# An encoder kernel: the up-projection's weight blocks, with one block staged in PSUM and eight plain slots at the head

## The reference, cut to what matters

```
def conv_gated_mlp(h, w_up, conv_w, conv_b, w_down):
    up = h @ w_up                                   # (512, 1024) @ (1024, 5632)
    conv = sum(pad(up)[:, j:j + s] * conv_w[j] for j in range(3)) + conv_b
    a, b = jnp.split(conv, 2, axis=-1)
    return (jax.nn.gelu(a) * b) @ w_down

x = x + conv_gated_mlp(rmsnorm(x, g_ffn[l]), w_up[l], conv_w[l], conv_b[l], w_down[l])
```

## Time and profile before

| what | us |
|---|---|
| median of 3 runs (lowest to highest) | 1777.44 (1775.38 to 1779.08) |
| the profiled execution's own time | 1771.03 |
| its span | 1769.2 |
| TensorE busy | 1690.7 (96%) |
| VectorE busy | 1157.3 (65%) |
| ScalarE busy | 853.9 (48%) |
| GpSimd busy | 892.2 (50%) |

### The profile page before, as it was taken

The page is one execution under the profiler, slowest core; times in us unless marked ns, Lnnn a source line. Parts: engine busy times, 40 slices in busy tenths (PEclk is TensorE's granted clock), DMA queues, the critical chain, the costliest instruction groups (busy, mean ns, idle before and its releaser), DMA issues. The chain is left out here.

```text
span 1769.2 us, 24563 instructions
## 1 busy us (share of the span) xinstructions
PE 1690.7 (96%) x9161; PEld 1467.7 (83%) x9161; DVE 1157.3 (65%) x1644; ACT 853.9 (48%) x1535; POOL 892.2 (50%) x784
## 2 busy tenths in 40 slices
PE   9999999999995999999999999999999859999998
PEld 7888888888875999988888888888888759999886
DVE  5778875433368899972146887745333788999822
ACT  5766743223353566652256756432224636666423
POOL 3433433333476788853343433334335668888522
PEclk9999999999997999999999999999999979999999
DMA  8322232223231222243252222222332412333332
GB/s 262 108 78 90 72 119 73 95 95 142 96 119 48 96 96 96 96 145 100 92 187 96 72 78 90 96 96 92 97 143 76 139 48 80 101 100 103 132 113 77
DMA packets 147319, 182.78 MB, mean 103 GB/s; under 512 B 3040, under 2 KB 130706, under 8 KB 146194
## 3 DMA queue, kind: packets, MB, share of 16 engines
q1 hardware_dynamic: 147090, 181.35, 30.7%
q10 hardware_dynamic: 128, 0.09, 0.0%
HBM read 170.92 MB, written 10.50 MB: 103 GB/s over the span
## 5 line engine op out<-in xcount | busy, mean ns | idle before, releaser
L616 POOL TENSOR_TENSOR w_lo<-raw,w_hi 128x256 fp32r<-128x256 f32 x596 | 472.9, 828 | 740.6 <-ACT w_hi L718 740.6
L1814 PE MATMUL banks<-xg_hi,w_hi 128*128 128x512 f32 x768 | 302.3, 394 | 9.4 <-DVE w_lo L1259 9.4
L1815 PE MATMUL banks<-xg_lo,w_hi 128*128 128x512 f32 x768 | 300.5, 391 | 0.0
L1816 PE MATMUL banks<-xg_hi,w_lo 128*128 128x512 f32 x768 | 300.2, 391 | 0.0
L1259 DVE TENSOR_TENSOR w_lo<-raw,w_hi 128x768 fp32r<-128x768 f32 (+2 forms) x110 | 97.3, 885 | 167.8 <-ACT w_hi L717 167.6
L666 POOL TENSOR_TENSOR s_lo<-s,s_hi 128x1024 fp32r<-128x1024 f32 x72 | 194.7, 2725 | 13.5 <-ACT s_hi L1024 13.5
L1814 PEld LDWEIGHTS banks<-xg_hi,w_hi 128*128 128x128 f32 x768 | 145.1, 189 | 40.2 <-DVE w_lo L1259 11.0
L2049 PE MATMUL banks<-h_set,s_hi 128*128 128x256 f32 x576 | 148.3, 289 | 28.3 <-ACT banks L1034 15.1
L1816 PEld LDWEIGHTS banks<-xg_hi,w_lo 128*128 128x128 f32 x768 | 144.9, 189 | 30.5
L1815 PEld LDWEIGHTS banks<-xg_lo,w_hi 128*128 128x128 f32 x768 | 145.2, 189 | 28.8 <-issue 0.2
L717 ACT ACTIVATE w_hi<-raw 128x768 fp32r<-128x768 f32 (+2 forms) x111 | 80.6, 726 | 174.8 <-PE banks L1816 86.0
(11 more groups left out here) (247 smaller groups left out, 4250.2 us busy)
## 6 DMA issues: line engine op xcount, KB each, us to landing
raw<-in_w_in SPq DMA_DIRECT2D x55, 1024.0 KB, 5.1
raw<-in_w_up SPq DMA_DIRECT2D x44, 1024.0 KB, 5.1
raw<-in_w_br SPq DMA_DIRECT2D x16, 1024.0 KB, 4.9
raw<-in_w_down SPq DMA_DIRECT2D x12, 1024.0 KB, 5.0
x_spill<-x_res SPq DMA_DIRECT2D x4, 2048.0 KB, 7.6
x_res<-x_spill SPq DMA_DIRECT2D x4, 2048.0 KB, 9.2
raw<-in_w_out SPq DMA_DIRECT2D x8, 1024.0 KB, 4.9
raw<-in_w_down SPq DMA_DIRECT2D x8, 896.0 KB, 4.6
```

What stands on the lines that cost most here:

```text
L616: last = nc.gpsimd.tensor_tensor(w_lo[p_][:, k, :], raw[p_][:, k, :], f32(w_hi[p_][:, k, :]), ALU.subtract)
L1814: nc.tensor.matmul(out, w_hi[w][:, k, cols], x_hi[:, a, :], start=first and k == 0, stop=False)
L1815: nc.tensor.matmul(out, w_hi[w][:, k, cols], x_lo[:, a, :], start=False, stop=False)
L1816: mm = nc.tensor.matmul(out, w_lo[w][:, k, cols], x_hi[:, a, :], start=False, stop=last and k == kt - 1)
```

## The change

Three things, all in the up-projection.

1. `NS` goes from 4 to 8: eight slots are plain and 14 are blocks.
2. In a block, ScalarE first copies a21 into PSUM bank 7 (`stage`). VectorE takes s3 = a11 - bank 7, then s1 in place in bank 7, s2 from it, and s4 as before with two operands in SBUF. The high part of s1 is a ScalarE pass of its own, 512 elements, from the bank; its low part is made by VectorE (`block_low`) instead of GpSimd. s2, s3 and s4 lie together: ScalarE's high part of them is one pass of 1536, GpSimd's low parts are passes of 512 and 1024. On ScalarE this pass now stands before `seed(z, 2)`.
3. At the head the product with rms stays in its bank (`up_bank`, banks 0 to 5 in turn), and the taps read PSUM. ScalarE writes rms a second time, into bank 7, and VectorE makes `h` in one operation per tile from x, the gain and that bank; ScalarE's eight gains and GpSimd's four passes of `normalise` are gone. The lists of all engines for the head are rewritten as loops over the eight slots.

```diff
-NS = 4
+NS = 8
...
+    s234 = [sb(f"s234_{i}", kb, [P, 12, P]) for i, kb in enumerate((66, 60, 167))]
...
+    def up_bank(n, half):
+        return bank[2 * (n % 3) + half]
+    STAGE = 7
...
-            normalise(0)
-            split(S_F + 2)
-            normalise(1)
-            split(S_F + 3)
-            block_lo(0, 0)
...
+            for s in range(S_F + 2, S_S):
+                split(s)
+                if s >= S_S - 3:
+                    operand_lo(H_POOL[s - S_S + 3])
+            for n in range(4):
+                block_lo(0, n)
...
+            def stage(z):
+                sc.wait_ge(raw_in[z % 2], l * SLOTS * 8 + 16 * ((S_S + z) // 2 + 1))
+                if z == 0:
+                    sc.wait_ge(h_ok, l * KT + KT)
+                else:
+                    sc.wait_ge(s1_low, l * SZ + z)
+                nc.scalar.activation(stage_bank(), raw[z % 2][:, 0:4, P:2 * P], ACT.Copy).then_inc(staged, 1)
...
+            for n in range(NS):
+                if n < NS - 1:
+                    split(S_F + n + 1)
+                if n == 0:
+                    round_sum(2 * l + 1)
+                    nc.scalar.preload_act_table_set(LN_EXP)
+                    norm_rms(2 * l + 1)
+                    nc.scalar.activation(bank[HEAD][:, :], ln_buf[:, :], ACT.Exp, scale=-0.5).then_inc(rms_p_ok, 1)
+                if n == NS - 1:
+                    stage(0)
+                for half in range(2):
+                    conv_centre(n, half)
+                    if n % 2 == 0:
+                        gelu(n // 2, half)
+                    if n == 3 and half == 0:
+                        for q in H_ACT[0:3]:
+                            operand_hi(q)
+                    if n == 4 and half == 0:
+                        for q in H_ACT[3:5]:
+                            operand_hi(q)
+                    if n == 4 and half == 1:
+                        for q in H_ACT[5:7]:
+                            operand_hi(q)
+                    if n == NS - 1 and half == 0:
+                        for b in range(4):
+                            block_hi(0, b)
+            stage(1)
             for z in range(SZ):
...
                     block_hi(z + 1, 0)
                     seed(z, 1)
                     block_hi(z + 1, 1)
+                    block_hi(z + 1, 2)
...
                 seed(z, 2)
                 if z < SZ - 1:
-                    block_hi(z + 1, 2)
                     block_hi(z + 1, 3)
...
+                if z < SZ - 2:
+                    stage(z + 2)
...
+            def evacuate(n, half):
+                ve.wait_ge(proj_done, proj_n(l, S_F + n, half))
+                nc.vector.tensor_tensor(up_bank(n, half), up_bank(n, half), rms[:, :], ALU.mult).then_inc(evacuated, 1)
+            def normalise(m):
+                ve.wait_ge(rms_p_ok, l + 1)
+                nc.vector.scalar_tensor_tensor(h[m // 4][:, m % 4, :], x_res[:, m, :], par[:, C_FFN + m:C_FFN + m + 1],
+                                               bank[HEAD][:, :], ALU.mult, ALU.mult).then_inc(h_ok, 1)
...
-                nc.vector.tensor_tensor(s1, a21, a22_, ALU.add).then_inc(s_add, 1)
-                nc.vector.tensor_tensor(s3, a11, a21, ALU.subtract).then_inc(s_add, 1)
-                ve.wait_ge(s_add, 4 * Z + 1)
-                nc.vector.tensor_tensor(s2, s1, a11, ALU.subtract).then_inc(s_add, 1)
+                nc.vector.tensor_tensor(s3, a11, stage_bank(), ALU.subtract).then_inc(s_add, 1)
+                nc.vector.tensor_tensor(stage_bank(), stage_bank(), a22, ALU.add).then_inc(s_add, 1)
+                ve.wait_ge(s_add, 4 * Z + 2)
+                nc.vector.tensor_tensor(s2, stage_bank(), a11, ALU.subtract).then_inc(s_add, 1)
...
+            def block_low(z):
+                Z, p = l * SZ + z, z % 2
+                ve.wait_ge(s_hi, 4 * Z + 2)
+                nc.vector.tensor_tensor(s1_lo[p][:, :, :], stage_bank(), f32(s1_hi[p][:, :, :]), ALU.subtract).then_inc(s1_low, 1)
...
+            for n in range(NS):
+                if n < NS - 1:
+                    split(S_F + n + 1)
...
+                for half in range(2):
+                    evacuate(n, half)
+                    if n == NS - 1 and half == 0:
+                        block_adds(0)
+                    if n == NS - 1 and half == 1:
+                        block_adds(1)
+                    convolve(n % 2, n // 2, half, up_bank(n, half).rearrange("p (r n) -> p r n", r=REQS))
+                    if n == 1:
+                        for m in range(2 * half, 2 * half + 2):
+                            normalise(m)
+                    if n == 2:
+                        for m in range(4 + 2 * half, 6 + 2 * half):
+                            normalise(m)
+                    if n == 3:
+                        for q in range(2 * half, 2 * half + 2):
+                            h_sum(q)
+                    if n in (4, 5):
+                        operand_lo(H_VECTOR[2 * (n - 4) + half])
+                    if n == NS - 1 and half == 0:
+                        block_low(0)
+            block_low(1)
             block_sums(0)
             for z in range(1, SZ):
...
                 for half in range(2):
                     convolve((z - 1) % 2, i, half, half_out(z - 1, half))
+                    if z < SZ - 1 and half == 0:
+                        block_low(z + 1)
...
+            for n in range(2, NS):
+                for half in range(2):
+                    if n > 2:
+                        pe.wait_ge(conv2_ok, conv_n(l, n - 3 - NS, half))
+                    feature_half(S_F + n, half, xg_hi, xg_lo, out=up_bank(n, half))
...
                 pe.wait_ge(s_hi, 4 * Z + 2)
+                pe.wait_ge(s1_low, Z + 1)
                 operand(1)
+                product(1, region(z, "m5"), s1_hi[p], s1_lo[p], True, None)
+                pe.wait_ge(s_hi, 4 * Z + 3)
                 pe.wait_ge(seeded, 3 * Z + 1)
                 operand(2)
+                product(2, region(z, "c12"), s234_hi[t][:, 0:4, :], s234_lo[p][:, 0:4, :], False, 2)
```

More of the change, by code:

```diff
@@ L213, in encoder_kernel @@
     g_lo = sb("g_lo", 151, [P, FT, N], F32R)
-    up = [sb(f"up{i}", 131 + 2 * i, [P, REQS, SEQ]) for i in range(2)]
     conv = [sb(f"conv{i}", 195 + 2 * i, [P, REQS, SEQ]) for i in range(2)]
-    act = [sb(f"act{i}", 199 + 2 * i, [P, REQS, SEQ]) for i in range(2)]
+    act = [sb(f"act{i}", 131 + 2 * i, [P, REQS, SEQ]) for i in range(2)]
     g_f32 = sb("g_f32", 151, [P, FT, N])
@@ L374, in conv_n, with stage_bank @@
         return l * 2 * (2 * FSLOT) + 2 * (NS + z) + half + 1
-    UP_BANK = ((0, 1, 2, 3), (4, 5, 7, 3))
+    def up_bank(n, half):
+        return bank[2 * (n % 3) + half]
+    STAGE = 7
+    def stage_bank():
+        return bank[STAGE].rearrange("p (k c) -> p k c", k=4)
     H_ACT = (0, 3, 5, 1, 2, 4, 6)
@@ L643, in _ @@
                     split(S_O + n)
[L644 to L649, removed]
             def operand_lo(q):
@@ L1029, in seed @@
                     sc.wait_ge(block_sum, 2 * (Z - 2) + 2)
-                if n == 0 and z < 2:
-                    sc.wait_ge(evacuated, evac_n(l, slot_evac(S_S + 2 * z - 4, 1)))
+                if n == 0 and z == 0:
+                    sc.wait_ge(conv2_ok, conv_n(l, -2, 1))
+                if n == 2 and z == 0:
+                    sc.wait_ge(conv2_ok, conv_n(l, -1, 0))
                 sc.wait_ge(block_done, 7 * Z + n + 1)
@@ L1509, in conv_count @@
                 return (l * FSLOT + i) * 4 + 2 * ab + half + 1
-            def evacuate(ab, i, half):
-                s = S_F + 2 * i + ab
-                if ab or i:
-                    ve.wait_ge(conv2_ok, conv_count(ab, i, half) - 2)
-                ve.wait_ge(proj_done, proj_n(l, s, half))
-                nc.vector.tensor_tensor(up[half][:, :, :].rearrange("p r n -> p (r n)"), bank[UP_BANK[i][2 * ab + half]],
-                                        rms[:, :], ALU.mult).then_inc(evacuated, 1)
+            def evacuate(n, half):
[5 more added lines that the diff above has]
+                                               bank[HEAD][:, :], ALU.mult, ALU.mult).then_inc(h_ok, 1)
             def convolve(ab, i, half, u):
@@ L2037, in _ @@
                 feature_half(S_F + 1, half, xg_hi, xg_lo)
-            for s in range(S_F + 2, S_S):
+            for n in range(2, NS):
                 for half in range(2):
-                    feature_half(s, half, xg_hi, xg_lo, out=bank[UP_BANK[1][2 * (s - S_F - 2) + half]])
+                    if n > 2:
+                        pe.wait_ge(conv2_ok, conv_n(l, n - 3 - NS, half))
+                    feature_half(S_F + n, half, xg_hi, xg_lo, out=up_bank(n, half))
             def blocks(z):
-                Z, p = l * SZ + z, z % 2
+                Z, p, t = l * SZ + z, z % 2, s_temp(z)
                 def product(q, out, hi, lo, first, low_ready):
```

146 lines of the change are left out of this document (34 added, 112 removed).

## The result

| what | us |
|---|---|
| before, median of 4 runs | 1776.41 (1775.38 to 1779.08) |
| after, median of 4 runs | 1734.25 (1733.78 to 1737.53) |
| ratio, 95% interval | 0.9764 (0.9747 to 0.9781) |
| the profiled execution: own time, span | 1733.78, 1732.0 |

A forecast was written before the change was run, and what follows sets the result against it. VectorE was taken as the bound in blocks and head. Per layer 115.6 + 13 x 11.1 + 0.3 = 260.2 us against 273.1, 26 saved in both layers, so a median of 1751; range 1727 to 1768.

The forecast's parts named there:

- The steady blocks: Blocks after the entry: gating products held, product 6 1.9 us late every second block, a pair 22.2 us against 21.85.
- the first rival: In gating blocks, the product gets in ahead of GpSimd's a1 pass: a pair takes 20.3 us, total 1727; chance 0.13.
- The blocks gain nothing: In the blocks, VectorE is no longer full but TensorE waits at product 6: a pair 22.2 us against 21.85.
- block 0: First block after the slots: 18.1 us, with product 1 2.1 late, 3.6 before seed 2, and 1.4 of halved clock.
- the port: Exclusion between GpSimd passes and VectorE operations with two SBUF operands; 5 us put in the head, 2.1 on block 1's sums.
- the head: Eight plain slots, bounded by VectorE's chain from rms: block 0 starts at 97.5 us, with 10 us of small waits.
- The two waits that I had chosen: In the head, VectorE waits 5 us for GpSimd's passes and 3 us for ScalarE's operand copies ahead of a split.
- the term of the fourteen halves: VectorE's chain in the head, slots 0 to 6: 14 halves of 1.6 us plus 1.56 for taps, 44.1 us.
- PSUM forms still wait for GpSimd: Rival in the blocks: no relief from PSUM operands, blocks of 11.54 us, total 1763; chance 0.03.
- The seed: Rival in the blocks: a held fourth sum moves seed 2 and product 4 back by up to 2.3 us, 1815; chance 0.07.
- The falling clock: Rival in the head: waits near 2 us drop the clock, five drops per layer cost 17 us, 1768; chance 0.12.
- The disputed price: VectorE's PSUM operands taken as costing no more than SBUF; by the skill's rule 0.065 us more each, 3.6 in all, 1755.

The follow-up runs named there:

- Experiments 1: Changed kernel, but in the blocks except the last the gating product takes a factor from the PSUM bank instead of act in SBUF: 1711.33 us.
- experiment 2: Changed kernel plus one wait: in odd blocks from 3 on, GpSimd's a1 pass waits for VectorE's first gating product; 1710.76 us, ratio 0.9650.
- experiment 3: Changed kernel with the old block form (no staging, all low parts on GpSimd), keeping eight slots and the new head: 1732.82 us, ratio 0.9776.
- Experiments 4 to 6: Old blocks and old normalisation: eight slots, up-projection in SBUF, 1762.72 us; eight slots, up-projection in bank, 1729.59; kernel before with only the up-projection in bank, 1749.91.
- experiment 4: Kernel before with eight plain slots and the rewritten head order; up-projection in SBUF, normalisation on GpSimd, old blocks: 1762.72 us, ratio 0.9959.
- experiment 8: Changed kernel with a wait before GpSimd's a1 pass in odd blocks from 3 on, for VectorE's first tap instead of its gating product: 1750.33 us.
- the wait alone: Kernel with the new head and old blocks, plus GpSimd's wait for the first gating product: 1747.88 us, against 1732.82 without the wait.
- the bank alone: Changed kernel, with staging in the PSUM bank, against the same new head with old blocks: 1734.25 us against 1732.82.
- experiment 9: Changed kernel with GpSimd's wait for the gating product, and block 0's staging, sums and two weight parts put forward: 1715.53 us, ratio 0.9691.

## Why the prediction was right, and what it got wrong

**The steady blocks** came out step by step. The sums are free, the first gating product is held (0.27 us behind the pass, 0.25 forecast), the second too, the gap is at product 6 in every second block (1.70; 1.9 forecast), the pair takes 22.19 (22.2). From block 1 to the end of the stage 144.1 us pass where the sum had 144.6. Experiments 1 and 2 show the cause, and the case of the first rival with its price (23.5 us; 24 between the forecasts). "The blocks gain nothing" is what experiment 3 measured: a difference of 1.4 us, the wrong way and within the noise.

**Where the rest lay.** The sum per layer was 260.2 and the stage takes 254.2. The step that failed is block 0: it was given 18.1 us and takes 14.4. Its first wait was right (2.1; 1.99), but product 4 waits 1.14 instead of 3.6. I had let the sums of block 1 lose the port by 2.1; the one with two SBUF operands, at 596.45, takes 0.69. And no halved clock stands behind it (1.4). That it was free was luck of the same kind: it started 0.10 us ahead of GpSimd's next pass.

```profile
596.45 0.69 DVE L1566 TENSOR_TENSOR s<-raw,s 128x512 f32<-128x512 f32 x1
```

```profile
596.55 2.84 POOL L664 TENSOR_TENSOR a_lo<-raw,a_hi 128x1024 fp32r<-128x1024 f32 x1
```

This time it is GpSimd's pass that is longer, 2.84 instead of the 2.40 of a free one. The second is the head: block 0 was forecast at 97.5 and starts at 95.6, with 6.7 us of gaps instead of 10. The two waits that I had chosen are there, about as chosen. For the port I had put 5: the eight sums and low parts of h take 13.1 us where the sum had 9.7 (one took 3.42 at 567.66, where a free one takes 1.2), and three weight parts some 0.5 to 0.6 more than free ones. For ScalarE I had put 3: VectorE waits 2.20 ahead of 562.26, and 0.7 more than in the other halves ahead of 557.39. What was sized too large is the term of the fourteen halves, 44.1, which take 42.4: the part ahead of the taps is 1.54 and not 1.6, and the two taps take 1.44 and not 1.56 where no gating product follows. With 0.5 from the steady blocks that is 6.0 a layer, 12 in all. The last 5 us of the miss on the median are no work at all: the profiled execution of before stood 6.4 under its median, that of after 0.5.

**What the forecast did not divide** is the head's gain. It was worked out as four blocks fewer and a head longer by 29.3, in which the free taps were hidden in the sum of a chain. Experiments 4 to 6 put the price on the parts: slots alone 9, the up-projection in its bank alone 25, both 42, normalisation on VectorE some -3.

**The rivals.** That PSUM forms still wait for GpSimd is refuted by the 690 ns, and by the two sums at 634.75 and 635.34 in the middle of a pass. The seed didn't fall behind: no gap stands at product 4 in the steady blocks. The falling clock was the nearest of them, in another place than I looked: not in the head, where no fall stands behind its gaps, but at the twelve gaps of product 6, which were 0.05 us shorter than those behind which it fell in experiment 8. So it is in part luck that the changed kernel kept its clock. Experiment 8 lost it and took 1750.3, by chance the time that was forecast.

**The disputed price.** The sums that read a bank take 676 to 692 ns and the one that reads two operands in SBUF 694, so the operand in PSUM costs nothing that these rows show. The rule that was set against it, of the Trainium skill (VectorE: DVE Perf Modes, section on the TRN2 errata), would by the prediction's estimate have made the PSUM forms 65 ns longer; the trace doesn't agree, and the sum rightly went without it.

## What to carry to other kernels

Find which of VectorE's operations read two operands in SBUF while GpSimd works, and where they stand in the chain that TensorE waits for; then either give one operand a place in PSUM or make GpSimd start behind the operation. Here the two went together: on top of the new head the wait alone cost 15 us, the bank alone 1 (noise), both brought 22. And when one operation is freed, look at who is now next to GpSimd's pass: here the gating product, and with that one free the sum s4 (850 ns in experiment 2, 694 in the changed kernel).

## What the runs showed of the hardware

- Gaps of TensorE of 1.69 to 1.71 us were followed by the full clock at all twelve places at product 6 in the changed kernel. Gaps of 1.75 to 1.76 at the same places, in experiment 8, were followed by a clock of about half at eleven of twelve. Single gaps of this length went either way. At slot 5 the changed kernel had 1.81 and 1.76 in its two layers, at product 1 of block 0 1.99 and 1.94, and the clock was 1.00 behind all four; in experiment 2 gaps of 1.80 and 1.94 at these two places had a fall behind them in layer 0, as the window behind the first shows:

```profile
552.00:554.00 2.00, 2.00 (x7) 1.52 (x6) 1.50 (x3) 0.43 (x1) 0.29 (x1) 0.50 0.25 39
```

  The longest that I find without a fall are 2.31 at slot 6 (experiment 9, layer 0; 2.28 there in layer 1 had one) and 2.83 at product 4 of block 0 (experiment 3, both layers). So from 1.75 to 2.83 us it went either way here, and a kernel whose repeated gap was 0.05 us longer took 16 us more. The length of the gap isn't all that decides; what else does was not tried.
- A held operation of VectorE ended some 0.55 us after GpSimd's pass did (0.54 to 0.56), whether sum (608.26 against 607.71 before), product (641.65 against 641.09 in the changed kernel) or tap (511.91 against 511.36 in experiment 4).
- The order of two operations 0.27 us apart, on two engines, twelve times over, set 23.5 us of the time (experiment 2).
